# Moving the fold's transfers to ScalarE, and the split of sixteen weight units from block 0 to block 1

## What is computed

```python
h = rms_norm(x, norm_g[l]) * (1.0 + scale[:, None, :]) + shift[:, None, :]
proj = h @ w_in[l]
u = proj[..., OFF_U:OFF_ZP]
z_pool = proj[..., OFF_ZP:OFF_Q]
pool_out = causal_pool_mixer(u, w_pool[l], ls_pool[l]) * jax.nn.silu(z_pool)
qk = jax.nn.silu(causal_depthwise_conv(proj[..., OFF_Q:OFF_V], conv_w[l], conv_b[l]))
o_gate = jax.nn.sigmoid(proj[..., OFF_O:OFF_ZM])
z_mlstm = proj[..., OFF_ZM:OFF_G]
hm = mlstm_chunkwise(q, k, v, ig, lf)   # then normed and scaled per head
mlstm_out = hm * o_gate * jax.nn.silu(z_mlstm)
mix = jnp.concatenate([pool_out, mlstm_out], axis=-1)
x = x + gate[:, None, :] * (mix @ w_out[l])
# in causal_pool_mixer: y = einsum('bsgc,gcd->bsgd', pooled, w_pool)
```

## Time and profile before

| | us |
|---|---|
| median of 3 runs | 1897.35 (1896.11 to 1897.38) |
| the profiled execution, device time | 1896.8 |
| its span, first to last instruction | 1894.7 |
| TensorE busy in the span | 1818.0 (96%) |
| VectorE, ScalarE, GpSimd busy | 1082.9, 469.2, 237.8 |
| mean granted TensorE clock | 0.995 of full speed |

### The profile page before, as it was taken

How to read it: one execution, slowest core, us unless ns; L and a number is a source line. 1 busy time by engine, 2 the same in 40 slices (tenths; PEclk the granted TensorE clock), 3 DMA queues, 4 the chain that set the end, 5 groups by cost and what they waited for, 6 DMA issues and landing times.

```text
span 1894.7 us, 25007 instructions
## 1 busy us (share of the span) xinstructions
PE 1818.0 (96%) x9505; PEld 1554.1 (82%) x9505; DVE 1082.9 (57%) x2453; ACT 469.2 (25%) x970; POOL 237.8 (13%) x213
## 2 busy tenths in 40 slices
PE   2797999999999999999999999999999999999998
PEld 1686888988888888988889888888889888898886
DVE  7677586454745367372764637544573727636373
ACT  1134432212322122121222122221221212222221
POOL 0443213000130002200030000300012000210000
PEclk9998999999999999999999999999999999999999
DMA  9598952656236652456425653265525564255521
GB/s 299 171 304 268 306 188 79 200 189 211 90 126 197 198 182 85 160 189 208 149 88 177 191 200 124 91 210 189 195 74 166 189 211 150 87 177 189 168 100 67
DMA packets 131483, 324.12 MB, mean 171 GB/s; under 512 B 11724, under 2 KB 49316, under 8 KB 131364
## 3 DMA queue, kind: packets, MB, share of 16 engines
q1 hardware_dynamic: 131364, 322.53, 51.8%
HBM read 276.28 MB, written 46.20 MB: 170 GB/s over the span
## 4 chain that ended last, share of the span: by engine, by line
PE 78%; DVE 10%; DMA 4%; issue 2%; ACT 1%; SPq 1%; POOL 0%; DVEq 0%; POOLq 0%
PE ps_acc L467 21%; PE ps_acc L469 21%; PE ps_acc L468 21%; DMA w_kept<-sb_w_split 3%; PE ps_kv L468 1%; PE ps_kv L469 1%; PE ps_kv L467 1%; PE ps_sco L626 1%; DVE sb_shifted L1433 1%; PE ps_num L480 1%; PE ps_num L654 1%; PE ps_kv L658 1%; PE ps_num L653 1%; DMA sb_w_raw<-w_in 1%; DVE sb_acc_cv L1433 1%
## 5 line engine op out<-in xcount | busy, mean ns | idle before, releaser
L467 PE MATMUL ps_acc<-sb_hT_hi,sb_w_split 128*128 128x512 f32 x1536 | 604.2, 393 | 0.0
L469 PE MATMUL ps_acc<-sb_hT_hi,sb_w_split 128*128 128x512 f32 x1536 | 600.1, 391 | 0.0
L468 PE MATMUL ps_acc<-sb_hT_lo,sb_w_split 128*128 128x512 f32 x1536 | 599.9, 391 | 0.0
L469 PEld LDWEIGHTS ps_acc<-sb_hT_hi,sb_w_split 128*128 128x128 f32 x1536 | 289.4, 188 | 61.6
L468 PEld LDWEIGHTS ps_acc<-sb_hT_lo,sb_w_split 128*128 128x128 f32 x1536 | 289.6, 189 | 59.4
L467 PEld LDWEIGHTS ps_acc<-sb_hT_hi,sb_w_split 128*128 128x128 f32 x1536 | 289.9, 189 | 58.1
L972 POOL TENSOR_TENSOR sb_h_rs<-sb_h_var,sb_mhalf 128x4 f32<-128x4 f32 x32 | 32.4, 1013 | 1129.0 <-DVE sb_h_var L1384 1129.0
L1292 DVE SCALAR_TENSOR_TENSOR sb_acc_cv<-sb_shifted,sb_par,sb_acc_cv 128x512 f32<-128x512 f32 x192 | 145.3, 757 | 6.8
L1318 DVE TENSOR_TENSOR sb_oz<-sb_tanh,sb_oz 128x512 f32<-128x512 f32 x32 | 22.2, 692 | 147.1 <-ACT sb_tanh L856 147.1
L467 PE MATMUL ps_acc<-sb_wo_hi,sb_mixm_hi 128*128 128x512 f32 x256 | 103.1, 403 | 0.0
L467 PE MATMUL ps_acc<-sb_wo_hi,sb_mixp_hi 128*128 128x512 f32 x256 | 100.6, 393 | 1.7 <-DVE sb_mixp_lo L1403 1.7
(11 more groups left out here) (220 smaller groups left out, 2956.8 us busy)
## 6 DMA issues: line engine op xcount, KB each, us to landing
sb_w_split<-w_kept SPq DMA_DIRECT2D x344, 512.0 KB, 3.6
sb_w_split<-w_kept SPq DMA_DIRECT2D x56, 520.0 KB, 4.0
w_kept<-sb_w_split SPq DMA_DIRECT2D x40, 512.0 KB, 5.6
sb_x_res<-x SPq DMA_DIRECT2D x34, 512.0 KB, 5.1
out<-sb_qT SPq DMA_DIRECT2D x32, 512.0 KB, 2.9
sb_x_in<-x SPq DMA_DIRECT2D x30, 512.0 KB, 5.3
sb_w_raw<-w_in SPq DMA_DIRECT2D x48, 256.0 KB, 4.3
w_kept<-sb_w_split SPq DMA_DIRECT2D x8, 520.0 KB, 4.7
```

Source lines behind the costliest of these rows:

```text
L467: pe.matmul(dst, st_hi, mv_hi, start=start, stop=False)
L468: pe.matmul(dst, st_hi, mv_lo, start=False, stop=False)
L469: return pe.matmul(dst, st_lo, mv_hi, start=False, stop=stop)
```

## The change

Units 24 to 39 (the z and o tiles) are still loaded raw and split in block 0, but no longer stored. In block 1 they are loaded raw and split a second time, and stored; block 2 is the first to load them split. The fold's first two loads are issued by SyncE with units 14 and 16, the other six by ScalarE at the end of tile t, after `fold_turn`. All of the fold's stores are issued by ScalarE, at the very start of its list for tile t = f + 9, and the last one behind the loop.

```diff
+KEEP_FIRST = [m for m in RAW_UNITS if m not in range(V_UNITS + 16, V_UNITS + 32)]
+KEEP_SECOND = list(range(V_UNITS + 16, V_UNITS + 32))
+KEEP_ORDER = KEEP_FIRST + KEEP_SECOND
...
-            def load_raw(m):
-
-                slot_free(0, m)
-                if m >= RING and m - RING in RAW_NO:
+            def load_raw(m, b=0):
+
+                slot_free(b, m)
+                if m - RING in (KEEP_FIRST if b == 0 else KEEP_SECOND):
                     kept_wait(m - RING)
...
             def load_fold(f):
 
-                if f >= 2:
-                    sp.wait_ge(fold_T, f - 1)
                 off = OFF_U + P * (f // 2)
...
                     if first:
-                        if m - RING + 1 in RAW_NO:
+                        if m - RING + 1 in KEEP_FIRST:
                             keep_w(m - RING + 1)
                         if m in RAW_NO:
                             load_raw(m)
...
-                        if m - 26 in range(2 * KT) and m % 2 == 0:
-                            load_fold((m - 26) // 2)
-                        if m - 33 in range(2 * KT) and m % 2 == 1:
-                            keep_fold((m - 33) // 2)
+                        if m in (14, 16):
+                            load_fold((m - 14) // 2)
+                    elif second:
+                        if m - RING + 1 in KEEP_SECOND:
+                            keep_w(m - RING + 1, 1)
+                        if m in KEEP_SECOND:
+                            load_raw(m, 1)
+                        else:
+                            if m - RING in KEEP_SECOND:
+                                kept_wait(m - RING)
+                            load_w(b, m)
...
+                def keep_fold(f):
+
+                    act.wait_ge(fold_lo, f + 1)
+                    for n, half in enumerate((mixm_hi, mixm_lo)):
+                        act.dma_start(w_kept[U_UNITS[f]][:, 512 * n:512 * n + 512],
+                                      half[:, f % 2, :, :].rearrange("p h t -> p (h t)").bitcast(F32)).then_inc(
+                            fold_kept[f % 2], 16)
...
                 for t, (name, i) in enumerate(TILES[:16]):
                     m = V_UNITS + 2 * t + 4
-                    if first:
-                        split_w(m)
+                    if first and 0 <= t - FOLD_TILE - 2 < 2 * NH:
+                        keep_fold(t - FOLD_TILE - 2)
+                    if first or second:
+                        split_w(m, b)
...
                     if first and 0 <= t - FOLD_TILE < 2 * NH:
                         fold_turn(t - FOLD_TILE)
-
+                        if t - FOLD_TILE + 2 < 2 * NH:
+                            load_fold(t - FOLD_TILE + 2)
+
+
+                if first:
+                    keep_fold(2 * NH - 1)
...
+                if second:
+                    for m in KEEP_SECOND:
+                        low_w(m, 1)
```

More of the change, by code:

```diff
@@ L260, in unit_used, with split_no @@
                     eng.wait_ge(acc_full, b * TASKS + (TASK[TILES[t]] + 1))
+        def split_no(b, m):
+            return RAW_NO[m] if b == 0 else len(RAW_UNITS) + KEEP_SECOND.index(m)
         def halves(m):
@@ L290, in kept_wait @@
             def kept_wait(m):
-                sp.wait_ge(w_kept_done[m % RING], 16 * len([n for n in RAW_UNITS if n % RING == m % RING and n <= m]))
-            def load_raw(m):
-                slot_free(0, m)
-                if m >= RING and m - RING in RAW_NO:
+                sp.wait_ge(w_kept_done[m % RING], 16 * ([n for n in KEEP_ORDER if n % RING == m % RING].index(m) + 1))
+            def load_raw(m, b=0):
+                slot_free(b, m)
+                if m - RING in (KEEP_FIRST if b == 0 else KEEP_SECOND):
                     kept_wait(m - RING)
@@ L328, in load_fold @@
                              w_in_v[:, 4 * (f % 2):4 * (f % 2) + 4, off:off + P]).then_inc(fold_loaded[f % 2], 16)
-            def keep_fold(f):
-                m = U_UNITS[f]
-                sp.wait_ge(fold_lo, f + 1)
-                for n, t in enumerate((mixm_hi, mixm_lo)):
-                    sp.dma_start(w_kept[m][:, 512 * n:512 * n + 512], t[:, f % 2, :, :].rearrange("p h t -> p (h t)").bitcast(F32)).then_inc(
-                        fold_kept[f % 2], 16)
             def load_x(nb, c, setup=False):
@@ L399, in _, with one_block @@
             sp.dma_start(fg[:, :], final_g.partition_broadcast(P)).then_inc(fg_loaded, 16)
-            def one_block(b, last, first=False):
+            def one_block(b, last, first=False, second=False):
                 wout_units = {V_UNITS + 2 * k + 4: k for k in range(KT)} if first else {}
@@ L515, in _, with one_block @@
             pe.wait_ge(setup_done, 1)
-            def one_block(b, last_block, first=False):
+            def one_block(b, last_block, first=False, second=False):
                 def acc_wait(name, i):
@@ L523, in w_wait @@
                 def w_wait(m):
-                    if first and m in RAW_NO:
-                        pe.wait_ge(w_lo_done, RAW_NO[m] + 1)
+                    if (first and m in RAW_NO) or (second and m in KEEP_SECOND):
+                        pe.wait_ge(w_lo_done, split_no(b, m) + 1)
                     else:
@@ L821, in fold_turn, with load_fold @@
                                    ACT.Copy).then_inc(fold_T_copied, 1)
+                def load_fold(f):
+                    off = OFF_U + P * (f // 2)
+                    act.dma_start(fold_raw[f % 2].rearrange("p (k n) -> p k n", n=P),
+                                  w_in_v[:, 4 * (f % 2):4 * (f % 2) + 4, off:off + P]).then_inc(fold_loaded[f % 2], 16)
+                def keep_fold(f):
[4 more added lines that the diff above has]
+                            fold_kept[f % 2], 16)
                 def fold_high(f):
@@ L841, in one_block @@
                         act.activation(shifted[:, t % 2, HALO:], src[:, :], ACT.Copy).then_inc(free, 1)
-                        if first:
-                            split_w(m + 1)
+                        if first or second:
+                            split_w(m + 1, b)
                         act.wait_ge(conv_done, b * 8 + (t + 1))
@@ L885, in m_high @@
                         act.wait_ge(acc_full, b * TASKS + (TASK["out", 2 * j - 3] + 1))
+                    elif first:
+                        act.wait_ge(fold_kept[j], 32 * NH)
                     act.activation(mixm_hi[:, j % 2, :, :], oz[:, :, chunk(j)], ACT.Copy).then_inc(m_hi, 1)
@@ L954, in _, with low_w @@
         def _(pool):
-            def low_w(m):
-                if m not in RAW_NO:
+            def low_w(m, b=0):
+                if m not in (RAW_NO if b == 0 else KEEP_SECOND):
                     return
-                pool.wait_ge(w_hi_done, RAW_NO[m] + 1)
+                pool.wait_ge(w_hi_done, split_no(b, m) + 1)
                 hi, lo = halves(m)
```

20 lines of the change are left out of this document (10 added, 10 removed).

## The result

The changed kernel took 1900.28 us (median of 20 executions, 1898.79 to 1902.77), the kernel before beside it 1897.44 (20 executions, 1895.34 to 1899.78): ratio 1.0014, 95% interval 1.0008 to 1.0021. That is +2.8 us, 0.15%, inside the 0.2% that I called the same, and 0.9 us above the 1899.4 forecast. The profiled execution of after took 1901.24 us with a span of 1899.3. Against the profile of before (1896.8) that is +4.4, more than the medians give: this profile is one of after's slower executions, and that of before one of its faster.

What follows compares the result with a forecast made beforehand. VectorE's list was taken as the bound behind TensorE's block 0 waits. R(0) 0.3, turns 1.1, clock 0.4 and block 1 0.3 gave +2.1 us on 1896.8: 1898.9 profiled, median 1899.4, range 1893.0 to 1905.0.

Steps and rivals of the forecast that it cites:

- The 5.8 us: TensorE's block 0 wait for the fold's first load: removing it gains 0 unless VectorE's first fold low part moves.
- R(0): End of VectorE's first fold low part in block 0: from 171.2 to 171.5 us, between 169.2 and 172.9.
- Step 2: Two early fold loads with units 14 and 16 delay later loads, splits and conv in block 0: +1.3 us, 0 to 1.7.
- Step 3: GpSimd's subtraction of unit 30 no longer runs beside wide_rows in block 0: -1.0 us, 0 to -2.
- The turns: Block 0, tiles 9 to 15: ScalarE and VectorE alternate, 7.2 us per z tile, 8.1 per o tile, 7.0 for tile 14.
- The price of the turns: Cost of ScalarE and VectorE alternating, to block 0's last product: +1.1 us, bounds -0.5 to +10.
- The clock: TensorE's slow stretch after its possibly longer wait in block 0: +0.4 us, 0 to 1.7.
- Block 1: Second split of sixteen units: GpSimd's subtractions slow VectorE up to z0, mostly absorbed by TensorE's room: +0.3 us, 0 to 4.
- Rival B: Issues from ScalarE cost more, or turns are longer: +6 us after block 0's first fold low part, 1905; chance 0.17.
- Rival C: Block 1 falls behind because its stores land slowly: +6 us, 1905; chance 0.08.
- Rival A: Stores and fold load bound block 0; first fold low part at 164.2, gain 5.6 us, 1891.7; chance 0.15.
- Rival D: TensorE's late wait before block 0's last chunk goes: -3.5 us, 1896; chance 0.08.

Runs made afterwards that it cites:

- the two pairs of profiles: Changed kernel and kernel before, each profiled a second time with no edit; second profiles 1901.38 us (changed) and 1896.98 us (before).
- the fold's half: Changed kernel with units 24 to 39 again stored in block 0 and loaded split in block 1: 1898.85 us, ratio 1.0012.
- the one without subtractions: Changed kernel, but in block 1 ScalarE copies the raw weight into the low half instead of GpSimd subtracting (output wrong): 1898.43 us, ratio 1.0006.
- the one with block 1's part alone: Changed kernel with all fold transfers issued by SyncE at their old places: 1897.74 us, ratio 1.0007.
- the four moves: Changed kernel, all units stored in block 0; two fold loads before block 0, R before wout_low and wout_scale, fold stores late, fold_turn(0) early: 1894.14 us.

## Why the prediction was right, point by point

- **The 5.8 us are worth 0.** Right. The fold's first load landed at 109.6 us, its wait is gone, and TensorE stood as long in the next place. That VectorE's list is what it waits for is shown by two experiments: put R(0) ahead of `wout_low` and `wout_scale`, or move the 5.9 us of `wide_rows` out from ahead of it, and the kernel gains; take traffic away (the sixteen stores) or bring the transposes' copy forward, and the medians show no gain.
- **The wait in its place was named wrongly.** I put 5 us or more on `sb_mixm_lo`; it was 6.6 on `sb_k_w` and 1.1 there. I had passed over the wait for `fold_turn(0)`: in before it was hidden behind the wait for the load, as its list position behind the tanh of k3 could have told me. Only 1.1 us of the product of step 1 hang on R(0) in after; the rest is this wait and the half-speed tile behind it.
- **R(0)**: 172.7, in 169.2 to 172.9, by two misses that cancel, so the number is in part luck. Step 2 (the early loads) was mis-sized: +1.3 with a top of 1.7, but SyncE's queue is 2.6 us later, and the product for k3 3.9 us in the first pair of profiles, 4.4 in the second. I had charged each load with its 0.87 us of the DMA engines only, not with 0.5 us of issue and with what a queue that is always a slot behind makes of it. Another 0.5 to 0.7 us lie in the conv of k3, beside which a subtraction now ran. Step 3 (GpSimd's subtraction off `wide_rows`) was too small: the way from the product for k3 to R(0) is 2.4 us shorter in the first pair and 1.7 in the second. In either pair all of `wide_rows` gave 2.0 (3.8 us for 5.7), the upper end of my bounds; in the first the `m_wide` group of four alone has 1.04 of it (1.13 against 2.17), and the product for k3 gave 0.68 more (0.69 against 1.37).
- **The turns**: right. 7.2 and 8.1 forecast, 7.3 and 8.0 measured. The last product starts 172.85 to 217.53 = 44.7 us after that of step 1; the forecast had 44.7 from R(0). Only the last turn is shorter (5.4, for 6.9 to 7.0), since TensorE's own 6.8 us are then the longer way. That they are from the order is shown: with the stores later, 6.8 to 6.9 each. One sign of the prediction failed and did not fit its own sum: ScalarE's tanh of tiles 12 and 13 came 1.4 us after the R before it, not 3; the terms ahead of it in the sum, 1.0 + 0.5 + 0.1, give 1.6.
- **The price of the turns** against before, forecast 1.1: 44.7 us against 214.75 - 171.35 = 43.4, so 1.3. With the 1.5 us by which R(0) and the product of step 1 are later it makes the 2.8 of the last product. Against a list in which nothing takes turns (late stores) it is 3.6. Before is slower than that list by 2.3 us, and 1.4 of them stand between the products of steps 1 and 2 (171.35 to 179.68, 8.3 us, against 6.9), where before runs at half speed after its wait for R(0).
- **The clock** (+0.4): the sign was wrong. The 6.6 us wait was followed by a half-speed stretch as the 5.8 us wait was, but the second drop, behind the wait for R(0) (171.0 to 174.4 us in before), did not come after a wait of 1.06 us. What that gave back, the 1.4 us just named, went into the turns.
- **Block 1** (+0.3, 0 to 4): +1.9, inside the bounds and mis-sized. I counted four subtractions at 0.9 us up to z0 and 4.0 us of room there. Up to z0 VectorE lost 2.7 us (409.94 - 356.47 against 404.45 - 353.71), 0.9 of it on a conv and 1.0 on a copy of 128x3. What I left out stands behind z0: `wide_rows`, 4.0 us longer, ahead of the product for z1. The Trainium skill (SBUF — State Buffer, section "SBUF: two separate sides") has VectorE operations with two SBUF inputs and GpSimd operations that read SBUF lock each other out for whole instructions, and the estimate by it was a wait of 1.4 us ahead of z2. The trace has 1.58 us ahead of z3, one tile later; that the two are near is luck. A group of four of `wide_rows` loses 0.9 to 1.0 us beside the subtractions, which is my 0.9 and not a whole 1.36, and GpSimd pays too: its four in a row took 6.13 us, 1.53 each.
- **Rival B** falls: ScalarE's two stores took 0.33 to 0.47 us each, less than SyncE's 0.43 and 0.50. **Rival C** falls: no wait for a split unit in block 1. **Rival A** falls: R(0) is at 172.7, and without the sixteen stores nothing was gained. (Its 164.2 should read 163.9: 171.2 less 6.3 and 1.0.) **Rival D**: the late wait of block 0 was 2.2 us in before and is 2.1 in after.
- **The sum**: +2.1 forecast, +2.8 by the medians, +4.6 and +4.7 by the two pairs of profiles. Of the 2.8 the block 1 term is 1.9 if the medians have it in full. That leaves 0.9 for block 0, where the profiles show 2.8. Why the medians show less there than two pairs of profiles stays open. The halves do not settle it: by the medians the two kernels with block 0's part alone (the fold's half, and the one without subtractions) are at +2.5 and +1.5 us, the one with block 1's part alone at +1.4, each with an interval of about 1.7 us to either side. That the forecast came within 0.9 us of the median owes something to this: the +2.1 is less than half of the +4.6 that the profiles show.

## What to carry to other kernels

A wait for a transfer can be taken away and be worth nothing: before that, follow the engine behind the next wait on the same consumer, and count the work in its list up to that point; here the kernels in which VectorE had less to do ahead of R(0) were the ones that gained (1.1 us against before in the changed kernel with R(f) put first, 6.3 with the four moves and `wide_rows` late). An instruction that waits, put at the head of another engine's list, makes the two engines take turns; the same instruction a few places later did not (3.6 us in the profile, hardly anything in the medians). Splitting work off to GpSimd is paid by VectorE while both run, so it belongs beside tiles in which VectorE has more room than the subtractions take.
